# Block doubling in a gated delta rule: the left product per head, as 64 by 64 in one half of the array's columns

## The reference

```
kk = einsum("nbhid,nbhjd->nbhij", k, k)
a_mat = where(strict, beta[..., :, None] * kk * decay, 0.0) + eye(CHUNK)
rhs = concatenate([v * beta[..., None], k * (beta * exp(gc))[..., None]], axis=-1)
sol = triangular_solve(a_mat, rhs, left_side=True, lower=True, unit_diagonal=True)
u, w = sol[..., :dv], sol[..., dv:]
...
def step(s, xs):
    v_new = u_c - einsum("bhck,bhkv->bhcv", w_c, s)
    o = einsum("bhck,bhkv->bhcv", qd, s) + einsum("bhij,bhjv->bhiv", qk_c, v_new)
    s = s * al[..., None, None] + einsum("bhck,bhcv->bhkv", kd, v_new)
```

## Time and profile before

| what | value |
|---|---|
| time, median of 3 runs | 2923.12 us (2918.58 to 2927.22) |
| the profiled execution's own time | 2930.31 us |
| its span, first to last instruction | 2928.4 us |
| mean granted TensorE clock | 0.97 |
| TensorE (PE) busy | 2729.6 us, 93% |
| weight loads (PEld) busy | 1754.6 us, 60% |
| VectorE (DVE) busy | 1463.8 us, 50% |
| ScalarE (ACT) busy | 633.4 us, 22% |
| GpSimd (POOL) busy | 159.0 us, 5% |

### The profile page before, as it was taken

The page is one execution under the profiler, slowest core; times in us unless marked ns, Lnnn a source line. Parts: engine busy times, 40 slices in busy tenths (PEclk is TensorE's granted clock), DMA queues, the critical chain, the costliest instruction groups (busy, mean ns, idle before and its releaser), DMA issues. The chain is left out here.

```text
span 2928.4 us, 36593 instructions
## 1 busy us (share of the span) xinstructions
PE 2729.6 (93%) x14042; PEld 1754.6 (60%) x14042; DVE 1463.8 (50%) x2848; ACT 633.4 (22%) x1354; POOL 159.0 (5%) x181
## 2 busy tenths in 40 slices
PE   6999899999999999889888899999799989899998
PEld 4888778889468888768635233333587544333332
DVE  4767567667356675465524232244544633234234
ACT  3132355556311110011322000000213421000000
POOL 0000222222000000000100000000000000000000
PEclk8999899999999999999999999999999999999999
DMA  6111354440223232222627999999322447999998
GB/s 262 58 57 66 113 178 151 145 145 16 92 72 88 88 88 84 79 74 72 231 104 292 407 417 418 418 418 418 113 72 102 129 190 302 418 416 417 418 418 353
DMA packets 112982, 614.91 MB, mean 210 GB/s; under 512 B 13008, under 2 KB 13472, under 8 KB 63008
## 3 DMA queue, kind: packets, MB, share of 16 engines
q1 hardware_dynamic: 102240, 576.68, 51.4%
q0 software_dynamic: 9120, 31.49, 3.0%
q10 hardware_dynamic: 1440, 4.29, 0.4%
HBM read 603.89 MB, written 8.51 MB: 209 GB/s over the span
## 5 line engine op out<-in xcount | busy, mean ns | idle before, releaser
L3078 PE MATMUL bank<-arena 128*32 128x512 f32 (+2 forms) x2048 | 432.3, 604 | 19.3 <-DMA arena<-in_w 18.4
L470 PE MATMUL bank<-arena 128*128 128x256 f32 x1776 | 411.9, 386 | 25.5 <-ACT arena L438 9.7
L470 PEld LDWEIGHTS bank<-arena 128*128 128x128 f32 x1776 | 339.6, 193 | 95.7 <-issue 29.1
L3078 PEld LDWEIGHTS bank<-arena 128*32 128x32 f32 (+2 forms) x2048 | 149.0, 135 | 275.2 <-issue 274.3
L3102 PE MATMUL bank<-arena 128*32 128x512 f32 (+2 forms) x1024 | 226.6, 643 | 27.6 <-DMA arena<-in_w 26.7
L3116 PE MATMUL bank<-arena 128*128 128x512 f32 x480 | 235.2, 613 | 5.7 <-DVE arena L3232 1.8
L3246 DVE SCALAR_TENSOR_TENSOR arena<-bank,arena 128x512 f32<-128x512 f32 x240 | 180.2, 751 | 79.6 <-PE bank L3116 66.7
L259 PE MATMUL bank<-arena 128*128 128x512 f32 (+1 forms) x608 | 210.0, 502 | 0.9 <-PEq L2540 0.9
L3102 PEld LDWEIGHTS bank<-arena 128*32 128x32 f32 (+2 forms) x1024 | 77.2, 140 | 173.7 <-issue 170.5
L3116 PEld LDWEIGHTS bank<-arena 128*128 128x128 f32 x480 | 76.5, 188 | 161.6 <-DVE arena L3246 96.6
L259 PEld LDWEIGHTS bank<-arena 128*128 128x128 f32 x608 | 114.9, 189 | 92.5 <-issue 85.4
(11 more groups left out here) (484 smaller groups left out, 3913.5 us busy)
## 6 DMA issues: line engine op xcount, KB each, us to landing
arena<-in_w SPq DMA_DIRECT2D x384, 1024.0 KB, 20.0
arena<-in_dense SPq DMA_DIRECT2D x308, 512.0 KB, 4.3
arena<-core_rows POOLq DMA_DIRECT2D x48, 256.0 KB, 5.4
arena<-in_xT SPq DMA_DIRECT2D x2, 2048.0 KB, 12.4
token_rows<-arena ACTq DMA_DIRECT2D x8, 512.0 KB, 4.8
gdn_gate<-arena POOLq DMA_DIRECT2D x8, 256.0 KB, 2.7
arena<-gdn_gate SPq DMA_DIRECT2D x1, 2048.0 KB, 7.7
arena<-band_bias POOLq DMA_DIRECT2D x2, 1024.0 KB, 6.1
```

The lines of the kernel that those rows point to most:

```text
L470: mm = pe.matmul(out, w[:, k, :], x[:, k, :], start=(k == 0), stop=(k == K1 - 1))
L3078: mm = pe.matmul(self.bank[2 + t][part, :], xT[i % 2][:, 2 * q + k, part], w[j][:, k, t, :], start=(q == 0 and k == 0), stop=(q == 3 and k ...
```

## The change

The left product is made per head: each 128 by 128 matmul becomes two of 64 by 64 (contraction still 128), for the columns 0 to 63 and 64 to 127 of the weights, which stand in one half of the array's columns each and write 64 partitions of PSUM each. The mask becomes two instructions on 64 partitions, each of which writes only its own diagonal block. `yn` gets a buffer of its own, whose other parts are zeroed once by GpSimd at the start of the stage; VectorE waits for that ahead of the first mask, and the waits for the old memsets count one more. To make room, the layout loses 96 unused columns, and buffers behind them shift.

```diff
-        self.core_free = f + 1536 + 5 * 96
+        self.core_free = f + 1536 + 4 * 96
...
-            b["yn"] = b["r"][:, 0:2, :]
+            b["yn"] = self.view(f + 16 if u else self.g_free + 1280, 2, P)
...
-        f += 16
+        f += 16 + 256
...
                             for q in range(2):
-                                mm = pe.matmul(Y[u][:, q, :], buf[u]["bl"][:, q, :], buf[u]["xl"][:, u, q, :],
-                                               start=True, stop=True)
+                                for c in (slice(0, 64), slice(64, P)):
+                                    mm = pe.matmul(Y[u][c, q, 0:64], buf[u]["bl"][:, q, c], buf[u]["xl"][:, u, q, c],
+                                                   start=True, stop=True)
                             mm.then_inc(s["y"], 1)
...
                     if p == 0:
-                        pe.wait_ge(s["zero"], 1)
+                        pe.wait_ge(s["zero"], 2)
...
+                for b in buf:
+                    last = pool.memset(b["yn"], 0.0)
+                last.then_inc(s["zero"], 1)
                 pool.memset(oT, 0.0)
                 pool.memset(S, 0.0).then_inc(s["zero"], 1)
...
                             dve.wait_ge(s["y"], 12 * p + 2 * (l - 1) + u + 1)
-                            dve.tensor_tensor(buf[u]["yn"], Y[u][:, 0:2, :], levels[:, l - 1, :, :].to_broadcast([P, 2, P]),
-                                              ALU.mult).then_inc(s["yn"], 1)
+                            if p == 0 and l == 1:
+                                dve.wait_ge(s["zero"], 1)
+                            for c in (slice(0, 64), slice(64, P)):
+                                last = dve.tensor_tensor(buf[u]["yn"][c, :, c], Y[u][c, 0:2, 0:64],
+                                                         levels[c, l - 1, :, c].to_broadcast([64, 2, 64]), ALU.mult)
+                            last.then_inc(s["yn"], 1)
...
                     if p == 0:
-                        dve.wait_ge(s["zero"], 1)
+                        dve.wait_ge(s["zero"], 2)
```

## The result

| | before | changed |
|---|---|---|
| time, median of 4 runs | 2923.71 us | 2946.84 us (2941.87 to 2949.66) |
| span of the profiled execution | 2928.4 us | 2947.7 us |
| mean granted TensorE clock | 0.97 | 0.97 |

The ratio is 1.0072, with a 95% interval of 1.0054 to 1.0089: the changed kernel is slower by 0.5 to 0.9%, 16 to 26 us. The forecast of 2938.5 us had the sign and the mechanism right and the size a third too small. The measured median lies inside the stated range of 2923 to 2949 us, and just above the band from half to one and a half times the sum (2946.8 against 2931 to 2946).

What follows compares the result with a forecast made beforehand. Rounds of the delta-rule core bound by a ring of waits through VectorE, or by TensorE's order; added 4.9 + 4.4 + 6.1 = 15.4 us, 2930.3 to 2945.7 profiled, less 7.2 for the median: 2938.5 us, range 2923 to 2949.

Steps and rivals of the forecast that it cites:

- one tile: Rounds 3 and 4 of pairs 0 to 8, with one modulation tile: +0.19 us each, from 3.28 to 3.47.
- empty: Rounds without other work beside them, late pairs: +0.41 us each, from 2.81 to 3.22.
- with gates: Rounds 4 and 5 of late pairs, where gate instructions L1259 and L1261 follow on VectorE: +0.51 us each.
- TensorE, the product: Left product as eight records in two parallel halves: load to result 0.44 us instead of 0.72.
- TensorE, the switch: Tiling switches around each left product: 0.74 us per chain from load to next load, against 0.66 before.
- VectorE, the masks: Two half masks on different start partitions don't overlap: 0.61 us until the copy starts, instead of 0.34.
- Chain 1's mask 1.44 (0.35 on): In a round without other work, the second recurrence's mask starts 0.35 us after the first's copy, at 1.44 us.
- What closes the rounds: VectorE's waits close empty and first rounds; TensorE's order closes one-tile rounds and rounds 2 and 5 of pairs 0 to 8.
- Overlapping masks: Rival: the two half masks overlap on VectorE, 0.41 us; +3 us, time 2926 us; chance 0.20.
- Freed TensorE time: Rival: TensorE's time counts and falls, switching free; 32 us saved, 2891 us, or 12 us, 2911 us; chance 0.10.
- A fallen clock: Rival: TensorE streams less in empty rounds and its clock falls; adds 11 us, time 2949 us; chance 0.03.
- Halves one after another: Rival: the product's halves run serially, 0.22 us more before each mask, up to 16 us, 2954 us; chance 0.02.

Runs made afterwards that it cites:

- e7_levels_low: The changed kernel, with the upper half's mask reading its mask values from the lower 64 partitions of the constant table; ratio to before 1.0059, stage 400.6 us.
- e3_two_full: The changed kernel's halved product, but the mask as two instructions over all 128 partitions by 128 elements each; ratio to before 1.0006, stage 387.3 us.
- e6_switch: The kernel before, with each left product laid out as two column halves by all 128 moving columns, mask unchanged; ratio to before 1.0084, stage 412.3 us.
- e1_product: The changed kernel with only the product in halves, the mask again one full instruction; ratio to before 0.9996, stage 385.7 us.
- e4_reversed: The changed kernel with the upper half's mask issued before the lower half's; ratio to before 1.0052, stage 396.7 us.

## Why the prediction was right, point by point

What the rounds became, in us against before (differences of the distances between chain 0's first loads in the traces; the last column is the change without the missed hold):

| rounds | forecast | changed | e7_levels_low |
|---|---|---|---|
| first, pair 0 | +0.70 | -0.18 | -0.37 |
| first, pairs 1 to 3 | +0.70 | +0.84 | +0.71 |
| first, pairs 4 to 11 | +0.36 | +0.61 | +0.49 |
| second, pairs 0 to 3 | +0.07 | +0.24 | +0.24 |
| one tile | +0.19 | +0.24 | +0.24 |
| fifth, pairs 0 to 8 | +0.07 | +0.10 | +0.10 |
| sixth, pairs 0 to 8 | 0 | -0.10 | -0.10 |
| empty (fourth, fifth of pair 11) | +0.41 | +0.58 | +0.45 |
| with gates (fourth, fifth of pairs 9, 10) | +0.51 | +0.68 | +0.45 |

- **TensorE, the product.** Forecast 0.44 us from load to result, measured 0.46; two halves side by side, eight records in 0.45 us. Right.
- **TensorE, the switch.** Forecast 0.74 us from one L1094 load to the next, measured 0.75 (676.31 to 677.06). "The two switches give back more than the array saves": e6_switch and e1_product put it at 27.4 given and 26.6 back, nearly even. Right. The Trainium skill, "TensorEngine Tiling (Array Packing)", Key Properties, says that TensorE drains when the tiling mode changes; the trace agrees with a gap of 0.20 us ahead of the first load. Of the speedup of up to 2x in that page's Theoretical Speedup no time was left.
- **VectorE, the masks.** Forecast that the second mask and the copy are held, 0.61 us until the copy starts; measured 0.62. Where the same elements start on partition 0 alone (e3_two_full) it is 0.41, and e4_reversed frees the copy by the order alone. Right, against the rival that had a chance of 0.20.
- **The mis-sized term.** "Chain 1's mask 1.44 (0.35 on)": the step from the copy to the next mask is 0.45 us, not 0.35. I had taken it from the earlier trace rows, where every instruction starts at partition 0, and had looked for held instructions only where the neighbour in the queue starts elsewhere. e7_levels_low shows that the last read of SBUF counts, two instructions back. The rule as the Trainium skill has it ("VectorE: DVE Perf Modes", Two Vector instructions with no wait between them) keeps the last start for each memory; by it the mask behind the copy is held too, and the trace agrees (0.45 us, and 0.34 in e7_levels_low). I used only half of it.
- **A misread row.** For the first round of the pairs 4 to 11 the prediction compares a load, 553.02, with 552.66, which in the earlier trace rows is the start of the product's first record. The load itself stands 0.11 us earlier:

```profile
552.55 0.53 PEld L1093 LDWEIGHTS bank<-arena 128*128 128x128 f32 x4
```

  So the term had to be +0.47 and not +0.36, eight times, 0.9 us in all. With the missed hold on top it is the +0.61 that was measured; without the hold, in e7_levels_low, it is +0.49.
- **What closes the rounds.** Right for the empty rounds, the one-tile rounds and the first rounds. Wrong for the second rounds of the pairs 0 to 3: both modulation tiles stand behind chain 0's product L1109 there, so that product waits for the masks as in a one-tile round. The round is 0.24 us longer, not 0.07. The sixth rounds of the pairs 0 to 8 have 128-column work behind them and so one switch less; they got 0.10 us shorter, where I had put nothing. The first round of the stage got 0.18 us shorter at its low clock, where I had put +0.70.
- **The sum.** 15.4 us forecast, 19.3 in the stage. The missed hold is some 3.4 us of the 3.9 between them. That the rest comes to only 0.5 us is luck: the misread row, the second rounds of the early pairs and a few hundredths in the others are some 3 us too low, and the stage's first round and the sixth rounds some 2.5 us too high.
- **The rivals.** Overlapping masks (+3 us, 2926): out for the change. e3_two_full, whose masks do overlap, bears out the price: its stage is 2.4 us longer, its time 2929.1 beside 2926.6 before. Freed TensorE time: out by e6_switch. A fallen clock: the stretch from 351 to 768 us shows a granted clock of 1.00. Halves one after another: out, eight records in 0.45 us.

## What to carry to other kernels

An edit that shortens work on the engine with the highest busy share (here TensorE, 98% in its stage) is worth only what the ring of waits lets through: find what closes the round first, and count every instruction that the edit adds on the other engines in that ring. Splitting a VectorE instruction by partitions was dearer here than splitting it by columns: 0.62 against 0.41 us until the next instruction, for two masks of 128 elements per partition. If a split by partitions is unavoidable, put last the half that starts where the following instructions start, or keep the SBUF inputs on one start partition; here the first was worth 7.5 us and the second 3.6, each tried by itself and not together.

Alone among 128-column work, a group of four matmuls in 64-column form paid 0.19 us for the switches, as much as it saved. What several such groups in a row would give, no run here shows.

## What the runs showed of the hardware

- VectorE held an instruction behind a full-width copy from PSUM for 0.45 us instead of 0.34, because of an SBUF operand two instructions before it; moving that operand from partition 64 to partition 0 undid it.
- A float32 record with 64 weight and 64 moving columns took 0.222 us from start to result in the trace, and eight of them in two halves 0.45 us. The first two records of each group, right behind the switch, last 0.27 us there.
- The first transpose load after a 64-column group comes 0.39 us after the group's first load (676.31 to 676.70) and 0.20 us after the start of the group's last one; before, that last step was 0.11 us. So the way out of the column form costs time as the way in does.
